# Two v projections as one group of seven block products in a two-layer gated trunk

## The reference

```python
h = rms_norm(x, norm_g[l])
proj = jnp.einsum('bsd,de->bse', h, w_in[l])
(a_u, a_v, a_z, b_q, b_k, b_v, b_z, i_q, i_k, i_w, g_a, g_b) = split_columns(proj)
y_a = spatial_gating_branch(jax.nn.gelu(a_u), jax.nn.gelu(a_v), a_z, ...)  # layer norm of v, mix over tokens
q = apply_rope(rms_norm(b_q.reshape(b, s, B_HEADS, B_HEAD_DIM), q_norm_g[l]), cos_q, sin_q)
k = apply_rope(rms_norm(b_k.reshape(b, s, B_HEADS, B_HEAD_DIM), k_norm_g[l]), cos_q, sin_q)
v = b_v.reshape(b, s, B_HEADS, B_HEAD_DIM)
att = sparse_attention_branch(q, k, v, qi, ki, i_w, topk)   # the 128 best keys by the indexer's score
merged = jax.nn.sigmoid(g_a + gate_b[l, 0]) * o_a + jax.nn.sigmoid(g_b + gate_b[l, 1]) * o_b
x = x + jnp.einsum('bsd,de->bse', merged, w_out[l])
```

## Time and profile before

| what | us |
|---|---|
| median of 3 runs | 781.27 |
| profiled execution | 781.41 |
| its span | 779.6 |
| TensorE busy | 769.0 (99%), 4412 matmuls |
| VectorE busy | 626.6 (80%) |
| ScalarE busy | 426.5 (55%) |
| GpSimd busy | 169.5 (22%) |

### The profile page before, as it was taken

One profiled execution on the slowest core, in us unless ns is written; L12 is line 12 of the kernel. 1 busy time (PEld: TensorE's weight loads), 2 busy tenths in 40 slices (PEclk: granted clock), 3 DMA queues, 4 the chain that ended last, 5 costly groups with the idle time before them and its releaser, 6 DMA issues.

```text
span 779.6 us, 12200 instructions
## 1 busy us (share of the span) xinstructions
PE 769.0 (99%) x4412; PEld 675.4 (87%) x4412; DVE 626.6 (80%) x1050; ACT 426.5 (55%) x790; POOL 169.5 (22%) x151
## 2 busy tenths in 40 slices
PE   7999999999999999999999999999999999999998
PEld 7988888888899889988899888888889998999886
DVE  5779999988768675779986798999887768746895
ACT  6566646342577447735564775643435773566342
POOL 1257511100130103012211674021012101110130
PEclk9999999999999999999999999999999999999999
DMA  9634237742796339685873522469148954577684
GB/s 333 227 113 130 82 108 146 168 119 82 148 154 190 81 78 147 201 234 111 191 240 102 170 82 82 135 139 213 55 88 171 175 163 63 111 142 225 164 148 123
DMA packets 54542, 113.67 MB, mean 146 GB/s; under 512 B 3537, under 2 KB 8849, under 8 KB 54481
## 3 DMA queue, kind: packets, MB, share of 16 engines
q0 software_dynamic: 22960, 47.27, 32.8%
q1 hardware_dynamic: 31232, 65.02, 25.9%
q10 hardware_dynamic: 288, 0.59, 0.2%
HBM read 97.14 MB, written 6.29 MB: 133 GB/s over the span
## 4 chain that ended last, share of the span: by engine, by line
PE 80%; DVE 7%; DMA 5%; ACT 4%; issue 3%; POOL 0%; SPq 0%; ACTq 0%; DVEq 0%; POOLq 0%
PE bank L858 15%; PE bank L860 15%; PE bank L859 15%; PE bank L926 5%; PE bank L928 5%; PE bank L927 5%; PE bank L979 5%; PE bank L832 2%; PE bank L850 2%; PE bank L895 2%; PE bank L896 2%; PE bank L897 2%; DVE w_lo L1426 2%; PE bank L788 1%; DMA g_a<-h_raw 1%
## 5 line engine op out<-in xcount | busy, mean ns | idle before, releaser
L1426 DVE TENSOR_TENSOR w_lo<-w_raw,w_hi 128x1024 fp32r<-128x1024 f32 x156 | 201.5, 1302 | 14.5 <-ACT w_hi L1064 8.8
L1064 ACT ACTIVATE w_hi<-w_raw 128x1024 fp32r<-128x1024 f32 x156 | 160.1, 1052 | 21.8 <-DMA w_raw<-in_w_out 15.1
L858 PE MATMUL bank<-w_lo,h_hi 128*128 128x512 f32 x256 | 100.5, 393 | 0.0
L860 PE MATMUL bank<-w_hi,h_hi 128*128 128x512 f32 x256 | 100.0, 390 | 0.0
L859 PE MATMUL bank<-w_hi,h_lo 128*128 128x512 f32 x256 | 99.9, 390 | 0.0
L732 POOL DMA_DIRECT2D w_raw<-in_w_in x32 | 38.6, 1207 | 237.8 <-DVE w_lo L1426 237.8
L926 PE MATMUL bank<-h_hi,w_lo 128*128 128x256 f32 x256 | 75.7, 296 | 0.0
L858 PE MATMUL bank<-h_lo,w_hi 128*128 128x512 f32 x192 | 75.3, 392 | 0.0
L860 PE MATMUL bank<-h_hi,w_hi 128*128 128x512 f32 x192 | 74.8, 390 | 0.0
L859 PE MATMUL bank<-h_hi,w_lo 128*128 128x512 f32 x192 | 74.8, 389 | 0.0
L928 PE MATMUL bank<-h_hi,w_hi 128*128 128x256 f32 x256 | 72.5, 283 | 0.0
(11 more groups left out here) (208 smaller groups left out, 1856.0 us busy)
## 6 DMA issues: line engine op xcount, KB each, us to landing
w_raw<-in_w_in SPq DMA_DIRECT2D x88, 512.0 KB, 4.3
w_raw<-in_w_in POOLq DMA_DIRECT2D x32, 512.0 KB, 6.0
w_raw<-in_w_out POOLq DMA_DIRECT2D x16, 512.0 KB, 6.4
w_raw<-in_w_out SPq DMA_DIRECT2D x12, 512.0 KB, 4.1
out<-x_sb POOLq DMA_DIRECT2D x4, 1024.0 KB, 5.5
w_raw<-in_w_oa SPq DMA_DIRECT2D x8, 512.0 KB, 3.3
w_raw<-in_w_ob SPq DMA_DIRECT2D x8, 512.0 KB, 4.2
x_sb<-out POOLq DMA_DIRECT2D x2, 2048.0 KB, 10.2
```

The costliest lines, as they stand in the source:

```text
L858: nc.tensor.matmul(dst, s_h, m_l, start=(n == 0), stop=False)
L860: last = nc.tensor.matmul(dst, s_h, m_h, start=False, stop=(n == len(pairs) - 1))
L1064: nc.scalar.activation(hi, w_raw[:, raw_slot(layer, u)], ACT.Copy).then_inc(s_whi.sem, 1)
L1426: nc.vector.tensor_tensor(lo, w_raw[:, raw_slot(layer, u)], hi.bitcast(F32), ALU.subtract) \
```

## The change

- vb and va become one group, v, of 14 jobs: the 1024 columns are vb and va side by side, and the output is token-major, 12 matmuls of 512 columns a job. ScalarE copies banks of a11, s5, s3 and a22 to `v_b` and `v_a`, VectorE adds those of a12, s6 and s4, and ScalarE takes the gelu of va's tiles as they are done (`VA_DONE`).
- The sums of h are made beside iq, k and q. s3 and s6 stay in SBUF for the gates; s5 and s4 are stored to a DRAM tensor `hold` and read back ahead of the gates, by SyncE.
- For k, ScalarE scales the tile by the reciprocal while it copies it; for q, the reciprocal with the attention scale is used as the scale of the exponential instead. The norms' weights are multiplied into tables of cosines and sines (`rope_g`) once a layer, so that GpSimd has one pass a tile.
- Top-8 rounds move to other slots; homes of weight blocks move between the regions. FILL, the mask's value, becomes -2^116.

The diff, cut to its core:

```diff
-    ("vb", "w_in", COL["vb"], 4), ("va", "w_in", COL["va"], 4), ("u", "w_in", COL["u"], 4),
+    ("v", "w_in", COL["vb"], 14), ("u", "w_in", COL["u"], 4),
...
+SEVENS = (V_G, GA_G, GB_G, OUT_G)
+HALF_COLS = {"v": (COL["vb"], COL["va"])}
...
-H_PARTS_AFTER = {JOB_VB[2]: 0, JOB_VB[3]: 1, JOB_VA[0]: 2, JOB_VA[1]: 3, JOB_VA[3]: 4, JOB_ZA[1]: 5}
+H_PARTS_AFTER = {JOB_IQ[3]: [0, 1], JOB_K[0]: [2, 3], JOB_K[2]: [4], JOB_K[3]: [5]}
-H_HI_AFTER = {JOB_ZA[3]: "s5", JOB_GA[0]: "s3", JOB_GA[2]: "s6", JOB_GA[4]: "s4"}
-H_LO_AFTER = {JOB_GA[1]: "s5", JOB_GA[3]: "s3", JOB_GA[5]: "s6", JOB_GA[7]: "s4"}
-TOPK_SLOTS = {10: [(1, 1)], 11: [(1, 1)], 12: [(1, 2)], 13: [(1, 2)], 14: [(1, 2)], 15: [(1, 3)], 16: [(1, 3)],
-              17: [(1, 2)], 18: [(2, 3)], 19: [(2, 3)], 20: [(2, 3)], 21: [(2, 3)], 22: [(2, 3)],
-              23: [(2, 1), (3, 1)], 24: [(3, 2)], 25: [(3, 2)], 26: [(3, 1)], 31: [(3, 1)], 39: [(3, 1)],
-              45: [(3, 1)], 46: [(3, 1)], 47: [(3, 2)], 49: [(3, 1)], 51: [(3, 2)], 53: [(3, 1)]}
+H_HI_AFTER = {JOB_V[0]: "s5", JOB_V[1]: "s3", JOB_V[2]: "s6", JOB_V[3]: "s4"}
+H_LO_AFTER = {JOB_V[1]: "s5", JOB_V[2]: "s3", JOB_V[3]: "s6", JOB_V[4]: "s4"}
+VA_DONE = {JOB_V[9]: 0, JOB_V[10]: 1, JOB_V[11]: 2, JOB_V[12]: 3}
+TOPK_SLOTS = {10: [(1, 2)], 11: [(1, 3)], 12: [(1, 1)], 13: [(1, 1)], **{n: [(1, 1)] for n in range(20, 26)}, 26: [(1, 3)],
+              27: [(2, 3)], 28: [(2, 4)], 29: [(2, 3)], 30: [(2, 1)], 31: [(2, 1)], 32: [(2, 2)], 33: [(2, 1)], 37: [(2, 1)],
+              **{n: [(3, 1)] for n in range(39, 53, 2)}, 46: [(3, 1)], 50: [(3, 1)], 52: [(3, 1)], 53: [(3, 2)],
+              55: [(3, 1)], 57: [(3, 2)], 59: [(3, 1)]}
...
-            if g in (GA_G, GB_G):
+            if g in (V_G, GA_G, GB_G):
                 return [UNIT_FIRST[g] + 4 + i for i, job in enumerate(LATE_GATE_UNITS[engine]) if job == j - FIRST_JOB[g]] + \
                     [UNIT_FIRST[g + 1] + i for i, job in enumerate(OB_UNITS[engine]) if job == j - FIRST_JOB[g]]
...
+                    if u in (UNIT_FIRST[V_G] + 8, UNIT_FIRST[V_G + 1]):
+                        i = int(u == UNIT_FIRST[V_G + 1])
+                        sp.wait_ge(s_hslo.sem, s_hslo.at(layer, H_ROUNDED.index(("s5", "s4")[i]) + 1))
+                        for j, part in enumerate(v_operand(("s5", "s4")[i])):
+                            sp.dma_start(hold[2 * i + j], part.bitcast(F32)).then_inc(s_hold[i].sem, 16)
+                    if u == UNIT_FIRST[GA_G] + 8:
+                        for i, name in enumerate(("s5", "s4")):
...
+                            for j, part in enumerate(gate_operand(name)):
+                                sp.dma_start(part.bitcast(F32), hold[2 * i + j]).then_inc(s_back[i].sem, 16)
...
+                def next_term(i):
+                    if i == 0:
+                        part_copied("-a22 lo beside")
+                        add_term("s5", 0, h_beside[:])
...
+                    if i == 5:
+                        pool.wait_ge(s_hterm["s5"].sem, s_hterm["s5"].at(layer, 48))
+                        add_term("s3", 1, h_sum_raw("s5"))
+                    if i == 6:
+                        pool.wait_ge(s_hterm["s3"].sem, s_hterm["s3"].at(layer, 32))
+                        add_term("s6", 1, h_sum_raw("s3"))
+                    if i == 7:
+                        part_copied("a22 hi to s4")
+                        add_term("s4", 0, h_sum_raw("s3"))
+                        add_term("s4", 1, bottom(h_lo, slice(HALF_K, KD)).bitcast(F32))
...
                 for n in range(2 * TILES):
-                    g_bc = kg_bc if n < TILES else qg_bc
-                    tile = stage[:, (TILES + n) % 2, 0:HEADS * DH].rearrange("p (h d) -> p h d", h=HEADS)
-                    pool.wait_ge(s_rinv.sem, s_rinv.at(layer, n + 1))
...
+                    next_term(n)
+                    pool.wait_ge(s_stage.sem, s_stage.at(layer, TILES + n + 1))
+                    times_cos_gains(TILES + n, n)
...
-                for g in (GA_G, GB_G):
+                for g in (V_G, GA_G, GB_G):
                     for u in range(UNIT_FIRST[g], UNIT_FIRST[g] + SEVEN):
                         if unit_adds(u):
                             add_weights(u)
...
+            def k_staged(layer, n):
+                t = n - JOB_K[0]
+                src, free = bank[bank_of(n)], s_free[bank_of(n)]
+                act.wait_ge(s_rinv.sem, s_rinv.at(layer, t + 1))
+                for h in range(HEADS):
+                    cols = slice(h * DH, (h + 1) * DH)
+                    act_.mark(nc.scalar.activation(stage[:, (TILES + t) % 2, cols], src[:, cols], ACT.Copy,
+                                                   scale=rstd[:, HEADS * t + h:HEADS * t + h + 1]))
```

More of the change, by code:

```diff
@@ L48 @@
 IDX_SCALE = ID ** -0.5 * IH ** -0.5
-FILL = -(2.0 ** 126)
+FILL = -(2.0 ** 116)
 TAKEN = -(2.0 ** 127)
@@ L124 @@
 OB_BANKS = [2, 0, 1, 2, 0, 1, 2, 0]
-JOB_GATES = JOB_GA + JOB_GB
+JOB_GATES = JOB_V + JOB_GA + JOB_GB
 def gate_of_job(n):
-    i, p = divmod(n - (JOB_GB if n in JOB_GB else JOB_GA)[0], 2)
+    i, p = divmod(n - next(jobs for jobs in (JOB_V, JOB_GA, JOB_GB) if n in jobs)[0], 2)
     return GATE_PRODUCTS[i], p
@@ L716, in _ @@
                 a21_hi, a21_lo = bottom(h_hi).bitcast(F32), bottom(h_lo).bitcast(F32)
-                part_copied("-a22 lo beside")
-                add_term("s5", 0, h_beside[:])
-                part_copied("a12 hi to s6")
-                add_term("s6", 0, top(h_lo, slice(HALF_K, KD)).bitcast(F32))
-                add_term("s5", 1, a21_hi)
-                part_copied("-a11 lo beside")
-                add_term("s3", 0, h_beside[:])
-                add_term("s5", 2, a21_lo)
-                pool.wait_ge(s_hterm["s5"].sem, s_hterm["s5"].at(layer, 48))
@@ new lines, in _ @@
+                for n in range(TILES):
+                    if n == 1:
+                        pool.wait_ge(s_xn.sem, s_xn.at(layer, TILES))
+                        pool.dma_start(stash[:, 2:4], x_sb[:, 2:4]).then_inc(s_stash2.sem, 16)
+                    pool.wait_ge(s_stage.sem, s_stage.at(layer, n + 1))
+                    b = ORDER[n]
+                    first = 0 if b else IH
+                    times_cos(n, stage[:, n % 2, first * ID:ROT_I], IH + 1 - first, ID, ci[:, b])
+                    if n == 2:
+                        gains_in_tables()
@@ L930, in gate_job_products, with v_job @@
                 last.then_inc(s_job.sem, 1)
+            def v_job(layer, n):
+                name, p = gate_of_job(n)
+                b = bank_of(n)
+                if takes_bank(n):
+                    pe.wait_ge(s_free[b].sem, s_free[b].at(layer, BANK_USE[n]))
+                elif name == "s3":
+                    pe.wait_ge(s_vsnap.sem, s_vsnap.at(layer, p + 1))
+                elif name == "s6":
+                    pe.wait_ge(s_vsnap.sem, s_vsnap.at(layer, 2 + p + 1))
+                elif name == "s4":
+                    pe.wait_ge(s_vsnap.sem, s_vsnap.at(layer, 4 + p + 1))
+                else:
+                    pe.wait_ge(s_vadd.sem, s_vadd.at(layer, 4 + p + 1))
+                if p == 0 and name in H_ROUNDED:
+                    pe.wait_ge(s_hslo.sem, s_hslo.at(layer, H_ROUNDED.index(name) + 1))
+                (w_hi, w_lo), w_k = block_home(V_G, name)
+                a_hi, a_lo = v_operand(name)
+                dst, tok = bank[b], slice(p * P, (p + 1) * P)
+                for k in range(HALF_K):
+                    if p == 0 and k % 2 == 0:
+                        pe.wait_ge(s_wlo.sem, s_wlo.at(layer, UNIT_FIRST[V_G] + 2 * PRODUCTS.index(name) + k // 2 + 1))
+                    wk, first = w_k.start + k, k == 0 and name in OPENS
+                    nc.tensor.matmul(dst[:], a_hi[:, k, tok], w_lo[:, wk], start=first, stop=False, skip_group_check=True)
+                    nc.tensor.matmul(dst[:], a_lo[:, k, tok], w_hi[:, wk], start=False, stop=False, skip_group_check=True)
+                    last = nc.tensor.matmul(dst[:], a_hi[:, k, tok], w_hi[:, wk], start=False, stop=(k == HALF_K - 1),
+                                            skip_group_check=True)
+                last.then_inc(s_job.sem, 1)
             def job(layer, g, j):
@@ L934, in job @@
                 n = FIRST_JOB[g] + j
-                if name not in ("oa", "ob"):
-                    w_hi, w_lo = weights(g)
                 b = bank_of(n)
@@ L1188, in evacuate @@
                 if n in JOB_OA + JOB_OB + JOB_OUT:
+                    return
+                if n in JOB_V:
+                    v_out(layer, n)
                     return
@@ L1584, in evacuate @@
             def evacuate(layer, n):
+                if n in JOB_V:
+                    v_added(layer, n)
+                    return
                 if n in JOB_GATES:
```

279 lines of the change are left out of this document (179 added, 100 removed).

## The result

The changed kernel takes 815.04 us (median of 4 runs, 812.65 to 816.15), the kernel before 781.25 beside it: a ratio of 1.0422, 95% interval 1.039 to 1.0454. The direction is as forecast, the size is not: 33.8 us more, where 19 were forecast, and 3 us above the range. The profiled execution took 816.15 us, with a span of 813.9.

A forecast was written before the change was run, and what follows sets the result against it. The kernel was taken as bound by matmuls issued one behind another. Per layer, +10.5 us in v and -1.0 later make +9.5, twice is +19 on the 781.41 us profiled: 800 us, range 783 to 812.

The forecast's parts named there:

- Matmuls: v group: 168 matmuls of 128x512 in place of 192 save TensorE 5.44 us a layer, 10.9 in all.
- k and q: k and q stages: ScalarE's added copies, some 8 us, stay hidden before the transposes; nothing charged to TensorE.
- The seam: From q to v: late s5 weight sums delay the first rounding to V0 + 14; TensorE stalls 11 us behind V1.
- VectorE's pace: V0 to V6: from t, the first s5 rounding's end, VectorE readies s3's second unit at t + 25.7; V6 ends t + 27.1.
- the rival in which the seam alone counts: v group: the seam stalls but VectorE keeps up, +1.1 to +5.4 us a layer, 782 to 790; chance 0.14.
- the one in which all is hidden: Seam at V1: the first s5 sum lands before about 92, so the wait vanishes, 768.5 us; chance 0.13.
- V7 to V13: End of v: seven unstalled jobs, 7 x 2.72 = 19.0 us, plus 0.4 for ws' transposes; no s4 or a22 load late.
- Later stages: Behind v: the s3 wait in the a gates goes, 1.0 us a layer; added top-8 rounds there are charged nothing.
- The allowance of 2 us a layer: a gates: margin of 2 us a layer for seven more top-8 rounds of 512 columns, which were charged nothing.
- The rival that named 812 to 817: Longer chain: accumulations of 8 to 10 us put t at V0 + 18, gates' attention steps lose 2 us; chance 0.08.

The follow-up runs named there:

- e9: Changed kernel with V10's and V11's bank adds ahead of u's weight remainders, and the top-8 rounds of ga8 and ga9 moved to oa: 807.31 us (1.0326).
- e10: Changed kernel with GpSimd's loads and terms reordered, and VectorE's rotation, remainders, index steps, top-8 rounds and bank adds reordered, same arithmetic: 779.03 us (0.9968).
- e12: e10 with three top-8 rounds moved to za (782.76 us), then the loads for units 4 and 5 put back behind q3's cosine pass: 795.80 us (1.0192).
- e2: Changed kernel with only s4's two terms moved, behind the loads for units 4 and 5: 806.49 us (1.0319).
- e3: Changed kernel with TensorE's gap behind V1 filled by 44 matmuls whose result nobody reads: 814.92 us (1.042).
- e5: Changed kernel with the loads for units 4 and 5 ahead of q3's cosine pass and s4's terms behind it: 796.10 us (1.0194).
- e4: Changed kernel without sums of weights in v: eight units become plain SyncE loads, so v is not the right product: 801.20 us (1.0241).
- e8: Changed kernel with only two top-8 rounds moved, ga12's to oa2 and one of oa5's two to oa4: 812.44 us (1.0404).

## Why the prediction was right in kind and short in size

**Matmuls.** The 5.44 us a layer are real: without a wait a job takes 2.72 us (e9), fourteen 38.1, where eight of twice the size took 43.5. e10 shows 3.1 and 2.6 of them in the time. That TensorE's busy time would fall was wrong in the changed kernel (772.4 for 769.0), which ran V2, V7 and, in layer 1, ga12 partly at the lower clock; it is right in e10 (762.2).

**k and q.** Charged at nothing, cost 0.5 us a layer, at k3. In q VectorE's busy time even fell from 25.37 to 17.80.

**The seam.** Right at each step. q2's pass ended at 86.9 (87.4 forecast), q3's at 96.3 (95.2 to 99.8), the first unit was rounded at V0 + 12.9 (14), TensorE resumed at 108.05 (108) after 10.3 us (11). e12 and e2 show that the load's place in the queue and s4's terms are its causes. That TensorE resumed just when forecast is partly luck: the first rounding ended 0.6 us ahead of the forecast 104.4, but the second was not right behind it, as ScalarE waited another 2.0 us for the second load.

**VectorE's pace.** Right: unit 9's remainder at t + 25.9 (25.7 forecast), V6's last matmul at t + 27.3 (27.1), and e2, e3 and e5 show the constant. It is also why the rival in which the seam alone counts (782 to 790) failed; the one in which all is hidden (768.5) failed at the seam.

**V7 to V13, the first step that failed.** I wrote that they are 7 x 2.72 = 19.0 us, 19.4 with ws' transposes, and "Of the loads for s4 and a22 none is late by this." They took 23.3 us in layer 0 and 22.5 in layer 1. VectorE subtracts unit 9, and only then can the sum for unit 13 be issued. GpSimd's issue of it, ScalarE's rounding, and VectorE's work behind:

```profile
130.08 1.21 POOL L817 DMA_DIRECT2D w_raw<-in_w_in  x1 [2.73 <-DVE w_lo L1575]
```

```profile
140.05 1.06 ACT L1178 ACTIVATE w_hi<-w_raw 128x1024 fp32r<-128x1024 f32 x1 [2.73 <-DMA w_raw<-in_w_in]
```

```profile
144.19 2.36 DVE L1575 TENSOR_TENSOR w_lo<-w_raw,w_hi 128x1024 fp32r<-128x1024 f32 x2 [0.25 <-ACT w_hi L1178]
...
147.44 0.69 DVE L1730 TENSOR_TENSOR v_a<-v_a,bank 128x512 f32<-128x512 f32 x1
...
151.19 0.69 DVE L1730 TENSOR_TENSOR v_a<-v_a,bank 128x512 f32<-128x512 f32 x1
```

The load issued at 130.08 took 9.9 us to land, so one load was late. It is the smaller part of the loss. The adds of V10's and V11's banks (L1730) stand behind u's remainders, and V12 and V13 wait for them, 1.0 and 0.7 us at the semaphore (0.3 and 0.7 in layer 1) and 2.2 with their late starts. In e4, where unit 13 came in time and was rounded right behind unit 12, the same waits are still 0.3 and 0.7 us in each layer:

```profile
PE bank L1038 <- DVEq L1731: 2.1, 4, 0.7
```

e9 took those 2.2 us away by order alone, though that rounding came only 1.8 us earlier and none of its followers had less to do: V7 to V13 took 19.7 us there, with V7 at full clock, and 20.5 in layer 1. Another 1.3 us was V7 at a clock of 0.65:

```profile
131.55:135.35 3.80, 3.80 (x13) 3.00 (x12) 2.38 (x2) 1.55 (x2) 0.00 (x0) 0.65 1.03 281
```

I had counted VectorE's work only up to unit 9 and let the rest run free. V7 started at V0 + 40.6, where the forecast has 41.1, and the stage came to +13.9 instead of +10.5.

**Later stages, the second one.** "leaves room, so I charge nothing": the wait at s3 did go (1.2 us), but ga took 2.0 and 3.5 us more than it would have without it. Both layers have the wait of 1.7 us at ga12, and in layer 1 ga12 then ran at a clock of 0.61 and took 4.4 us instead of 2.9:

```profile
663.10:667.50 4.40, 4.40 (x24) 4.40 (x25) 3.25 (x8) 3.16 (x7) 0.00 (x0) 0.61 0.71 227
```

The room was real in the sum over the stage (38.59 of 47.28 busy; I had said 39.2) and absent where a bank add stood behind two rounds and two remainders; e9, which takes the two rounds away, brings ga to 45.3 us. The slots of oa hold the same rounds as before the change, and it still took 1.0 and 0.3 us more. Of this 0.7 in layer 0 goes away in e8 and e9, which move rounds; the cause of the other 0.3 in each layer is open. The allowance of 2 us a layer should have been the charge.

Together: 2 x 3.4 in v, 2.8 and 3.6 in ga and oa (I had -1.0 each), 0.5 twice in k and 0.7 in out are the missing 15 us. The rival that named 812 to 817 had the right sum and half of the cause: its lost 2 us in the attention stages were there, but t was V0 + 12.9 and not V0 + 18, as only single loads took 8 to 10 us (the second at the seam 9.4, unit 13's 9.9). Line 817, accumulating weight loads, after (the earlier trace rows before):

```profile
DMA to landing us min/median/max: 5.7/6.2/9.9
```

The median of 6.2 us is the same as before the change, and again far from the 3.2 us that one works out, as an estimate, from the Trainium skill (DMA: Bandwidth & Descriptors, Anatomy of one DMA — SWDGE (gpsimd) path). The trace decides; with 3 us less, by the same estimate, the gap of 10.3 us would have been about a third shorter. Whether the accumulation or the transfers beside it make the difference, no run here separates.
